# Mask products of the stick-breaking attention issued one step early, ahead of the scores they are added to

## The chip, the cores and the metric

The kernel runs on one core of one Trainium2 chip. The metric is the device time of one execution in microseconds (us), the median of several runs; lower is better.

## The reference

One residual block of a streaming encoder: 1024 tokens, width 1024, all in float32. A mixing sub-layer (retention and stick-breaking attention side by side, gated, projected and merged) is followed by a squared-ReLU MLP. Only the stick-breaking part matters here: 8 heads of 64, in blocks of 128 queries.

```python
z = jnp.einsum('bthd,bshd->bhts', q[:, t0:t1], k[:, :t1]) * scale
valid = s_idx[None, :] < t_idx[:, None]
log_1m = jnp.where(valid, -jax.nn.softplus(z), 0.0)
log_stick = lax.cumsum(log_1m, axis=3, reverse=True) - log_1m
a = jnp.where(valid, jnp.exp(jax.nn.log_sigmoid(z) + log_stick), 0.0)
outs.append(jnp.einsum('bhts,bshd->bthd', a, v[:, :t1]))
```

A query sees only earlier keys, so the 128x128 square on the diagonal needs a mask, and no other square does.

## The kernel before

The kernel is written engine by engine, each engine with its own program, and semaphores between them. The order in which TensorE works is written out by hand. In the stretch from about 59 to 313 us it works through the stick-breaking attention and, between its small products, through the dense projections that produce q, k, v and the gate (`stick_tile`, lines 610 to 612: three float32r products of 512 or 256 columns for each of 8 chunks).

**Units.** Two heads are taken together (a group G, 4 of them). For each group the 8 query blocks make 12 units: query blocks 0 to 3 are one unit each, and blocks 4 to 7 are two each, first the unit with the four newest key blocks (it holds the diagonal), then the rest. So 32 of the 48 units are diagonal (numbers 0, 1, 2, 3, 4, 6, 8, 10 of each group of 12) and 16 are not.

**Score banks.** The two heads of a unit U write PSUM banks (2U) mod 3 and (2U+1) mod 3. The second of these was last used by the first head of unit U-1. ScalarE reads a bank twice, L1051 (sigmoid of -z into `uu`) and L1052 (sigmoid of z into `sg`), and each read raises `sg_done` by one. `scores(U)` waits for `sg_done >= 4U-2`: both reads of the first head of the unit in front.

**One step U on TensorE:** transposes of the weights of unit U-2 (L645, waits for the product L1444 of VectorE, `a_done`), scores of unit U (L627, three passes of two row-tiled products, 64 rows each), for a diagonal unit the mask (L633: identity times a bfloat16 mask of 0 and -1e30, a full 128x128 product of 128 columns for each head, added onto the last 128 columns of the scores; it raises `z_done`), then the dense projection work that `STICK_BESIDE` lists for this step, then attention times v of unit U-2 (L663, 128x64 column tiles, waits for ScalarE's copy L1044, `at_ready`). `STICK_BESIDE` has no entry for steps 11, 23, 35 and 47: there times-v follows the scores at once. Steps 12, 24 and 36 open a new group.

**The other engines in a step.** ScalarE: copy of the finished output (L1039), copy `aT` (L1044), the four sigmoids of unit U, then evictions of dense tiles and the rounding of weight pieces (L973). VectorE: two scans (L1438, they wait for `sg_done`) and the product L1444. GpSimd computes the low parts of weight pieces (L449).

Of the kernel before, what the change touches and what calls it, by code (L numbers as in the profile page):

```python
# [8 lines left out]
P = 128  # L9
# [62 lines left out]
UNITS = tuple(u for i in range(T) for u in ([(i, 0, i + 1, True)] if i < 4 else [(i, i - 3, i + 1, True), (i, 0, i - 3, False)]))  # L72
N_UNITS = len(UNITS)
ALL_UNITS = 4 * N_UNITS
# [9 lines left out]
TILE_AT = {t: n for n, t in enumerate(STICK_TILE)}  # L84
# [3 lines left out]
LOW_AFTER = tuple(sum(t[0] in "qk" for t in STICK_TILE[:n]) for n in range(len(STICK_TILE) + 1))  # L88
# [63 lines left out]
def build_block(nc, x, wstream, ada, ada_rows, smalls, pos, ident, maskd, dprime, adab, postg, out, m1_dram, mods, x2_dram):  # L152
# [4 lines left out]
    with ctx:  # L157
        def sem(name):
            return ctx.enter_context(nc.semaphore(name))

        def sb(name, shape, dt, c=ctx):
            return c.enter_context(nc.sbuf_tensor(name, shape, dt))
# [47 lines left out]
        with ExitStack() as c:  # L210
# [9 lines left out]
            id_b = sb("id_b", [P, P], bf16, c)  # L220
            msk_b = sb("msk_b", [P, P], bf16, c)
# [51 lines left out]
        def chunk_bank(u):  # L273

            return ps[:, 2 + u % 6 if u < 8 else 4 + (u - 8) % 3, :]

        def x_slot(i):

            return xs[:, (i + 4) % T, :]
# [13 lines left out]
        def z_bank(x, w):  # L293

            return ps[:, x % 3, 0:w]
# [14 lines left out]
        qk_low, ada_half = sem("qk_low"), sem("ada_half")  # L310
        z_done, sg_done, scan_done, a_done = sem("z_done"), sem("sg_done"), sem("scan_done"), sem("a_done")
# [212 lines left out]
        def _(pe):  # L524
            def tile(outp, lhs, rhs, chunks, sem=gemm_done, ready=None):

                for k in range(chunks):
                    if ready:
                        pe.wait_ge(*ready(k))
                    (lh, ll), (rh, rl) = lhs(k), rhs(k)  # L530
                    nc.tensor.matmul(outp, lh, rh, start=(k == 0), stop=False)  # L531
                    nc.tensor.matmul(outp, lh, rl, start=False, stop=False)  # L532
                    last = nc.tensor.matmul(outp, ll, rh, start=False, stop=(k == chunks - 1))  # L533
                last.then_inc(sem, 1)
# [31 lines left out]
            def x_transposed(u):  # L566

                th, c = divmod(u, KC)
                if u in (0, 8):
                    pe.wait_ge(n1_x, 4 * (th + 1))  # L570
                if u in (6, 7):
                    pe.wait_ge(n1_split, 2 * (u - 5))
                if u >= 11:
                    pe.wait_ge(n1_split, 2 * (u - 2))
                for q in range(4):
                    last = nc.tensor.transpose(chunk_bank(u)[:, q * P:(q + 1) * P],
                                               x_slot(4 * th + q)[:, c * P:(c + 1) * P], id_f[:, :])
                last.then_inc(n1_tr, 1)
# [35 lines left out]
            def scores(U):  # L614

                G, k = divmod(U, N_UNITS)
                i, b0, b1, diagonal = UNITS[k]
                w = (b1 - b0) * P
                if k in (0, 4):
                    pe.wait_ge(qk_low, LOW_AFTER[TILE_AT["k", G, k // 4] + 1])  # L620
                if U:
                    pe.wait_ge(sg_done, 4 * U - 2)
                hi, lo = qk_hi[G % 2], qk_lo[G % 2]
                for n, (a, b) in enumerate(((hi, hi), (lo, hi), (hi, lo))):
                    for h in range(2):
                        rows_ = slice(64 * h, 64 * h + 64)
                        last = nc.tensor.matmul(z_bank(2 * U + h, w), a[rows_, 0, i * P:(i + 1) * P], b[rows_, 1, b0 * P:b1 * P],  # L627
                                                start=(n == 0), stop=(n == 2 and not diagonal))
                        if n == 2 and not diagonal:
                            last.then_inc(z_done, 1)  # L630
                if diagonal:
                    for h in range(2):
                        nc.tensor.matmul(z_bank(2 * U + h, w)[:, w - P:w], id_b[:, :], msk_b[:, :], start=False, stop=True).then_inc(z_done, 1)  # L633

            def weights_transposed(U):

                _, b0, b1, _ = UNITS[U % N_UNITS]
                pe.wait_ge(a_done, U + 1)
                if U:
                    pe.wait_ge(at_ready, U)  # L640
                for n in range(2 * (b1 - b0)):
                    h, b = divmod(n, b1 - b0)
                    for r in range(2):
                        part = slice(64 * r, 64 * r + 64)
                        last = nc.tensor.transpose(px[:, r, 64 * n:64 * n + 64], sg[part, U % 2, h, b * P:(b + 1) * P], id_f[part, part])  # L645
                        if n == 2 * (b1 - b0) - 1:
                            last.then_inc(at_tr, 1)
# [21 lines left out]
            def stick_tile(n, k0=0, k1=KC):  # L669

                kind, at, tok = STICK_TILE[n]
                piece = 3 * (at // 2) + 2 * (at % 2) if kind in "qk" else 3 * at + 1 if kind == "v" else PC_GATE
                slot = piece % 2
                if k0 == 0:
                    pe.wait_ge(w_split, 4 * piece + 4)
                    if n >= 4:
                        pe.wait_ge(*((ev_act, EA_STICK + n - 1) if STICK_TILE[n - 2][0] in "va" else (qk_low, LOW_AFTER[n - 1])))
                for k in range(k0, k1):
                    if kind == "v":
                        l, r_ = ((a[:, k, tok * P:(tok + 1) * P] for a in (a_hi, a_lo)), (w[:, slot, k * 256:(k + 1) * 256] for w in (w_hi, w_lo)))  # L680
                    else:
                        m, th = ("qk".index(kind), tok) if kind in "qk" else TT[tok]
                        l, r_ = ((w[:, slot, k * 256 + m * P:k * 256 + (m + 1) * P] for w in (w_hi, w_lo)),
                                 (a[:, k, th * HALF:(th + 1) * HALF] for a in (a_hi, a_lo)))
                    last = passes(tile_bank(n)[:, 0:256 if kind == "v" else HALF], *l, *r_, k == 0, k == KC - 1)
                if k1 == KC:
                    last.then_inc(gemm_done, 1)

            def gate_tile(j):

                m, th = TT[j]
                pe.wait_ge(w_split, 4 * (PC_GATE + 1) + 4)
                if j < 3:
                    pe.wait_ge(sg_done, 4 * ALL_UNITS - 4 + 2 * j)
                else:
                    pe.wait_ge(ev_act, EA_GATE + 3)
                tile(pg[:, j, :], lambda k: tuple(w[:, 1, k * 256 + m * P:k * 256 + (m + 1) * P] for w in (w_hi, w_lo)),
                     lambda k: tuple(a[:, k, th * HALF:(th + 1) * HALF] for a in (a_hi, a_lo)), KC)
# [6 lines left out]
                    x_transposed(6 + k)  # L705
            for u in CHUNKS_AFTER[1]:
                x_transposed(u)
            for U in range(ALL_UNITS + 2):
                if U == 2:
                    pe.wait_ge(n1_split, 32)  # L710
                if U >= 2:
                    weights_transposed(U - 2)
                if U < ALL_UNITS:
                    scores(U)
                for n, k0, k1 in STICK_BESIDE.get(U, ()):
                    stick_tile(n, k0, k1)
                    for u in CHUNKS_AFTER.get(n, ()):
                        x_transposed(u)
                if U >= ALL_UNITS:
                    gate_tile(U - ALL_UNITS)  # L720
                if U >= 2:
                    times_v(U - 2)

# [9 lines left out]
            for g in range(GATE_G):  # L733
                ea, ev = EA_GATE + 8 * g, EV_GATE + 8 * g
                n = PC_GATE + 3 * g
# [14 lines left out]
            def ret_group(g, sub, it):  # L750
# [41 lines left out]
                pe.wait_ge(ev_act, ea + 8)  # L792
                pe.wait_ge(w_split, 4 * (n + 2) + 4)
                scores(0)
                for i in range(T):
                    if i < T - 1:
# [1068 lines left out]
```

## Time and profile before

| | us |
|---|---|
| median of 3 runs (1763.54 to 1768.31) | 1764.07 |
| the profiled execution, its own time | 1766.35 |
| its span in the profile | 1764.5 |
| TensorE matmul busy (9968 products) | 1708.8 |
| VectorE busy | 906.4 |
| GpSimd busy | 602.3 |
| ScalarE busy | 560.7 |

The profile is one execution, taken by the hardware profiler. PE is TensorE's matmuls, PEld its weight loads, DVE VectorE, ACT ScalarE, POOL GpSimd. Lxxx is a line of the kernel. Matmuls overlap in the pipeline, so that the duration of one (start to modelled end) is longer than the distance from one start to the next, and it is mostly the distance that counts. The granted clock of TensorE is 0.99 of full speed over the span.

### The profile page before, as it was taken

The numbers are of one execution on the slowest core, as the hardware profiler recorded it, in microseconds if no ns is written. First come the engines' busy times: TensorE is split into PE (matmuls) and PEld (weight loads), VectorE is DVE, ScalarE is ACT, GpSimd is POOL, SyncE is SP. The second block draws the span as 40 slices with busy tenths as digits, with TensorE's granted clock in tenths as the row PEclk, the third lists the DMA queues.
The fourth block names the chain that finished last, engine by engine and source line by source line (L and its number), as shares of the span: only waits on it lengthen the run. The fifth ranks groups of instructions, "written<-read, shape, count | busy, mean of one in ns | idle before, by whom it ended". The sixth has DMA issues, their size and how long they took to land.

```text
span 1764.5 us, 25435 instructions
## 1 busy us (share of the span) xinstructions
PE 1708.8 (97%) x9968; PEld 1422.3 (81%) x9968; DVE 906.4 (51%) x1284; ACT 560.7 (32%) x949; POOL 602.3 (34%) x256
## 2 busy tenths in 40 slices
PE   4999999999999999999999999899999999999997
PEld 3877877777989898978888997788888888888876
DVE  6757666776456555542113277636261616253526
ACT  4556666110121212120002175333333333323232
POOL 2012111343332322323333742553535353444420
PEclk8999999999999999999999999999999999999999
DMA  9001001255401111113111545111111112020112
GB/s 362 1 25 49 18 32 61 96 203 168 147 28 49 37 40 45 39 42 124 45 46 48 187 160 179 48 48 49 48 59 36 61 35 71 24 85 16 66 77 114
DMA packets 38159, 135.16 MB, mean 77 GB/s; under 512 B 5940, under 2 KB 6836, under 8 KB 37560
## 3 DMA queue, kind: packets, MB, share of 16 engines
q1 hardware_dynamic: 30240, 109.66, 18.3%
q10 hardware_dynamic: 7832, 24.28, 3.7%
q8 instruction: 62, 1.02, 0.2%
q14 instruction: 25, 0.20, 0.0%
HBM read 121.33 MB, written 12.60 MB: 76 GB/s over the span
## 4 chain that ended last, share of the span: by engine, by line
PE 90%; DVE 5%; issue 1%; ACT 1%; DMA 1%; SPq 1%; POOL 0%; POOLq 0%; ACTq 0%; DVEq 0%
PE ps L533 17%; PE ps L531 17%; PE ps L532 16%; PE ps L906 5%; PE ps L908 5%; PE ps L907 5%; PE ps L610 3%; PE ps L611 3%; PE ps L612 3%; PE ps L786 2%; PE ps L663 2%; PE ps L788 2%; PE ps L787 2%; PE ps L627 1%; PE ps L645 1%
## 5 line engine op out<-in xcount | busy, mean ns | idle before, releaser
L438 POOL TENSOR_TENSOR w_hi<-raw,zero 128x1024 fp32r<-128x1024 f32 x58 | 114.3, 1970 | 468.1 <-PE ps L533 272.1
L533 PE MATMUL ps<-r_hi,w_lo 128*128 128x512 f32 x640 | 254.3, 397 | 0.0
L531 PE MATMUL ps<-r_hi,w_hi 128*128 128x512 f32 x640 | 252.2, 394 | 2.1 <-issue 2.1
L532 PE MATMUL ps<-r_lo,w_hi 128*128 128x512 f32 x640 | 252.0, 394 | 0.0
L531 PE MATMUL ps<-w_hi,a_hi 128*128 128x256 f32 x768 | 219.2, 285 | 1.3 <-POOL w_lo L467 0.7
L533 PE MATMUL ps<-w_hi,a_lo 128*128 128x256 f32 x768 | 215.7, 281 | 0.0
L532 PE MATMUL ps<-w_lo,a_hi 128*128 128x256 f32 x768 | 215.5, 281 | 0.0
L472 POOL TENSOR_TENSOR w_lo<-w,w_hi 128x1024 fp32r<-128x1024 f32 x39 | 100.0, 2564 | 221.3 <-ACT w_hi L1222 221.3
L1714 DVE TENSOR_TENSOR m<-m,ps 128x512 f32<-128x512 f32 x208 | 136.4, 683 | 71.2 <-PE ps L908 70.7
L906 PE MATMUL ps<-w_hi,f_hi 128*128 128x512 f32 x392 | 156.2, 398 | 4.8 <-issue 3.7
L907 PE MATMUL ps<-w_lo,f_hi 128*128 128x512 f32 x392 | 156.0, 398 | 0.0
L908 PE MATMUL ps<-w_hi,f_lo 128*128 128x512 f32 x392 | 155.9, 398 | 0.0
L531 PEld LDWEIGHTS ps<-w_hi,a_hi 128*128 128x128 f32 x768 | 144.9, 189 | 2.7 <-POOL w_lo L467 0.9
L440 POOL TENSOR_TENSOR w_lo<-raw,w_hi 128x1024 fp32r<-128x1024 f32 x58 | 144.8, 2497 | 4.5
L532 PEld LDWEIGHTS ps<-w_lo,a_hi 128*128 128x128 f32 x768 | 144.9, 189 | 0.2
L531 PEld LDWEIGHTS ps<-r_hi,w_hi 128*128 128x128 f32 x640 | 120.1, 188 | 30.7 <-issue 2.3
L533 PEld LDWEIGHTS ps<-w_hi,a_lo 128*128 128x128 f32 x768 | 144.7, 188 | 0.0
L532 PEld LDWEIGHTS ps<-r_lo,w_hi 128*128 128x128 f32 x640 | 120.1, 188 | 30.3
L533 PEld LDWEIGHTS ps<-r_hi,w_lo 128*128 128x128 f32 x640 | 120.1, 188 | 28.6
L1438 DVE TENSOR_TENSOR_SCAN uu<-uu 128x512 f32<-128x512 f32 (+7 forms) x96 | 96.1, 1042 | 77.1 <-ACT uu L1051 76.8
L1701 DVE TENSOR_TENSOR f_lo<-hid,f_hi 128x1024 fp32r<-128x1024 f32 x35 | 51.8, 1480 | 151.4 <-ACT f_hi L1249 151.4
L449 POOL TENSOR_TENSOR w_lo<-raw,w_hi 128x1024 fp32r<-128x1024 f32 x16 | 42.9, 2689 | 235.1 <-ACT w_hi L973 235.1
(232 smaller groups left out, 3427.8 us busy)
## 6 DMA issues: line engine op xcount, KB each, us to landing
raw<-wstream SPq DMA_DIRECT2D x112, 512.0 KB, 3.7
ada_r<-ada_rows SPq DMA_DIRECT2D x32, 512.0 KB, 4.9
w<-wstream SPq DMA_DIRECT2D x32, 512.0 KB, 3.7
ada_s<-ada SPq DMA_DIRECT2D x7, 1024.0 KB, 17.3
m_dram<-m1s ACTq DMA_DIRECT2D x1, 4096.0 KB, 15.6
m<-m_dram ACTq DMA_DIRECT2D x1, 4096.0 KB, 12.2
x_dram<-m ACTq DMA_DIRECT2D x8, 512.0 KB, 4.3
rl_f<-x_dram ACTq DMA_DIRECT2D x2, 2048.0 KB, 10.3
```

What stands on the lines that cost most here:

```text
L438: nc.gpsimd.tensor_tensor(w_hi[:, slot, part], raw[:, h, :], zero[:, 0:1].broadcast_to([P, RAW]), ALU.add).then_inc(w_split, 1)
L440: nc.gpsimd.tensor_tensor(w_lo[:, slot, part], raw[:, h, :], w_hi[:, slot, part].bitcast(f32), ALU.subtract).then_inc(w_split, 1)
L472: return nc.gpsimd.tensor_tensor(out_, in0, in1, op)
L531: nc.tensor.matmul(outp, lh, rh, start=(k == 0), stop=False)
L532: nc.tensor.matmul(outp, lh, rl, start=False, stop=False)
L533: last = nc.tensor.matmul(outp, ll, rh, start=False, stop=(k == chunks - 1))
L610: nc.tensor.matmul(outp, hi, r_hi_, start=start, stop=False)
L906: nc.tensor.matmul(banks[:, t, :], fh, wh, start=(start and c == 0), stop=False, skip_group_check=not start)
L907: nc.tensor.matmul(banks[:, t, :], fh, wl, start=False, stop=False, skip_group_check=not start)
L908: last = nc.tensor.matmul(banks[:, t, :], fl, wh, start=False, stop=(c == 1), skip_group_check=not start)
L1438: V.tensor_tensor_scan(run, run, run, 1.0, ALU.mult, ALU.bypass).then_inc(scan_done, 1)
L1714: V.tensor_tensor(dst, dst, bank, op).then_inc(ff_ev, 1)
```

## The change

Four things are edited. The mask products of a diagonal unit move out of `scores` into a function of their own, `mask_first`. They now open the accumulation in the bank (`start=True`, only in the last 128 columns), and the scores are added to them (`start=False` for a diagonal unit). `mask_first(U + 1)` is called in step U behind the dense work and in front of `times_v(U - 2)`; `mask_first(0)` stands ahead of the loop. The wait for `sg_done` goes with the mask: for a diagonal unit it now stands in `mask_first`, and the scores no longer have it. `z_done` of a diagonal unit is now raised by the last pass of the scores. Numbers of products, columns and operands are the same.

```diff
@@ scores(U)
-                if U:
+                if U and not diagonal:
                     pe.wait_ge(sg_done, 4 * U - 2)
...
                         last = nc.tensor.matmul(z_bank(2 * U + h, w), a[rows_, 0, i * P:(i + 1) * P], b[rows_, 1, b0 * P:b1 * P],
-                                                start=(n == 0), stop=(n == 2 and not diagonal))
-                        if n == 2 and not diagonal:
+                                                start=(n == 0 and not diagonal), stop=(n == 2), skip_group_check=diagonal)
+                        if n == 2:
                             last.then_inc(z_done, 1)
+
+            def mask_first(U):
+
+                _, b0, b1, diagonal = UNITS[U % N_UNITS]
+                w = (b1 - b0) * P
                 if diagonal:
+                    if U:
+                        pe.wait_ge(sg_done, 4 * U - 2)
+                    else:
+                        pe.wait_ge(qk_low, LOW_AFTER[TILE_AT["k", 0, 0] + 1])
                     for h in range(2):
-                        nc.tensor.matmul(z_bank(2 * U + h, w)[:, w - P:w], id_b[:, :], msk_b[:, :], start=False, stop=True).then_inc(z_done, 1)
+                        nc.tensor.matmul(z_bank(2 * U + h, w)[:, w - P:w], id_b[:, :], msk_b[:, :], start=True, stop=False, skip_group_check=True)
@@ the loop over steps
+            mask_first(0)
             for U in range(ALL_UNITS + 2):
...
                 if U >= ALL_UNITS:
                     gate_tile(U - ALL_UNITS)
+                if U + 1 < ALL_UNITS:
+                    mask_first(U + 1)
                 if U >= 2:
                     times_v(U - 2)
```

## Rows read from the trace of the kernel before

**Rows 1.** The page: the chain of work that ended last, by engine.
```profile
PE 90%; DVE 5%; issue 1%; ACT 1%; DMA 1%; SPq 1%; POOL 0%; POOLq 0%; ACTq 0%; DVEq 0%
```

**Rows 2.** Windows (one group's stretch): start:end, length, busy us by engine, PEclk, DMA share, GB/s.
```profile
133.00:193.00 60.00, 59.52 (x570) 47.25 (x568) 41.56 (x46) 36.92 (x80) 9.11 (x4) 1.00 0.12 36
```

**Rows 3.** Waits of PE, 55 to 340 us: waiting line, releaser, us in total, times, longest.
```profile
PE ps L645 <- DVE sg L1444: 2.3, 3, 1.7
PE ps L610 <- POOL w_lo L449: 1.9, 1, 1.9
PE ps L663 <- ACT aT L1044: 0.7, 4, 0.2
```

**Rows 4.** Line L633, the mask: durations in ns min/median/max, first and last start.
```profile
L633 PEld LDWEIGHTS ps<-msk_b,id_b x64: 95/97/99, 59.8 to 306.6; 128*128 128x128 bf16 x64
L633 PE MATMUL ps<-msk_b,id_b x64: 219/224/230, 59.8 to 306.7; 128*128 128x128 bf16 x64
```

**Rows 5.** Timeline of PE, step 8 (diagonal, 512 columns beside): start us, duration us, instruction.
```profile
116.20 0.40 PE L627 MATMUL ps<-qk_lo,qk_hi 64*128 64x512 f32 x2
116.53 0.29 PE L633 MATMUL ps<-msk_b,id_b 128*128 128x128 bf16 x2
...
119.29 0.39 PE L612 MATMUL ps<-a_hi,w_lo 128*128 128x512 f32 x1
119.61 0.66 PE L663 MATMUL ps<-aT,vs 128*64 128x128 f32 x8
```

**Rows 6.** Timeline of PE, step 9 (not diagonal, 512 columns beside).
```profile
121.34 0.34 PE L627 MATMUL ps<-qk_lo,qk_hi 64*128 64x384 f32 x2
...
124.28 0.40 PE L612 MATMUL ps<-a_hi,w_lo 128*128 128x512 f32 x1
```

**Rows 7.** Timeline of PE, steps 7 (not diagonal) and 22 (diagonal), 256 columns beside.
```profile
111.54 0.28 PE L627 MATMUL ps<-qk_lo,qk_hi 64*128 64x256 f32 x2
...
114.44 0.28 PE L611 MATMUL ps<-w_lo,a_hi 128*128 128x256 f32 x1
114.56 0.28 PE L612 MATMUL ps<-w_hi,a_lo 128*128 128x256 f32 x1
114.76 0.44 PE L663 MATMUL ps<-aT,vs 128*64 128x128 f32 x4
...
186.40 0.40 PE L627 MATMUL ps<-qk_lo,qk_hi 64*128 64x512 f32 x2
...
189.61 0.28 PE L612 MATMUL ps<-w_hi,a_lo 128*128 128x256 f32 x1
```

**Rows 8.** Timeline of all engines, step 11, which has no dense work beside.
```profile
131.36 0.81 ACT L1044 ACTIVATE aT<-ps 128x768 f32<-128x768 f32 x1 [0.24 <-PE ps L645]
131.65 0.40 PE L627 MATMUL ps<-qk_lo,qk_hi 64*128 64x512 f32 x2
132.22 0.88 PE L663 MATMUL ps<-aT,vs 128*64 128x128 f32 x12 [0.17 <-ACT aT L1044]
132.58 0.59 ACT L1052 ACTIVATE sg<-ps 128x512 f32<-128x512 f32 x1
133.03 0.71 PE L645 MATMUL ps<-id_f,sg 64*128 64x64 f32 x16
133.55 0.31 PE L627 MATMUL ps<-qk_hi 64*128 64x128 f32 x2
```

**Rows 9.** Timeline, step 12: ScalarE's second read, and the last dense product.
```profile
136.18 0.34 ACT L1052 ACTIVATE sg<-ps 128x128 f32<-128x128 f32 x1
...
137.46 0.40 PE L612 MATMUL ps<-a_hi,w_lo 128*128 128x512 f32 x1
```

**Rows 10.** Timeline of PE, step 13: the transposes of unit 11 wait for VectorE.
```profile
139.18 0.71 PE L645 MATMUL ps<-id_f,sg 64*128 64x64 f32 x16 [0.30 <-DVE sg L1444]
```

**Rows 11.** Windows behind the two longest idle times of PE in the stretch.
```profile
100.00:104.00 4.00, 3.91 (x11) 3.10 (x12) 1.06 (x3) 0.00 (x0) 0.04 (x1) 0.58 0.43 131
...
322.00:325.00 3.00, 2.71 (x25) 2.29 (x26) 0.23 (x1) 1.03 (x1) 0.00 (x0) 1.00 0.00 0
```

## The prediction

> **What bounds the kernel now.** I read the chain of waits first: 90% of the chain that ended last is TensorE's own work, so what counts is TensorE's issue time, and other engines only where TensorE waits for them [rows 1]. Next the windows over the attention stretch: in one group's 60 us TensorE has matmuls in flight for 59.52 us, VectorE is busy for 41.56 and ScalarE for 36.92 [rows 2]. Then TensorE's waits there: 4.9 us in all, of which the 1.9 us for a weight piece and 1.7 us of the 2.3 for VectorE are two single events [rows 3]. So there is almost no stall that an earlier mask could remove. What is left is the price of the mask on TensorE itself, at its old and at its new place, and the wait that moves with it. Nothing behind about 323 us is touched by the change; it only starts later or earlier.
>
> **The mask at its old place (removed).** The 64 products last 224 ns each [rows 4], but what they cost is the distance that they put between neighbours. In a diagonal step from the end of the scores (116.20 + 0.40 = 116.60) to the start of the last dense product (119.29) it is 2.69 us [rows 5]; in a step without mask and with the same 12 dense products it is 124.28 - (121.34 + 0.34) = 2.60 us [rows 6]. That is 0.09 us for both heads. With 24 dense products of 256 columns: 189.61 - 186.80 = 2.81 against 114.56 - 111.82 = 2.74, or 0.07 us [rows 7]. It is this cheap because the array is emptied between row-tiled scores and full-array work with or without the mask, and the mask goes in where that has already been paid. Taken: 32 units x 0.08 = **-2.6 us**.
>
> **The mask at its new place (added).** No trace has it there, so I build it from neighbours. Dense products of 256 columns start 0.12 us apart, and from the last of them to times-v, which uses the array in another shape, it takes 0.20 us: its duration less about 0.08 [rows 7]. With 512 columns it is 119.61 - 119.29 = 0.32 against a duration of 0.39, so 0.07 less [rows 5]. The exit costs the last product's duration less 0.07, whatever that product is. With the mask behind the dense work: one spacing to the first mask product (0.12), 0.07 to the second (a pair takes 0.29 for 0.22 each [rows 4, 5]), then the exit, 0.22 - 0.07 = 0.15. Sum 0.34 against 0.20, and without rounding 0.13 us more. With 512 columns the same 0.13, for spacing and exit grow alike. The first product of the kernel's mask, ahead of the loop, costs the pair and the exit, 0.07 + 0.15 = 0.22 us. There are 28 steps in which `mask_first(U + 1)` stands behind dense work: 28 x 0.13 + 0.22 = **+3.9 us**. Bounds: not under the 0.07 that the pair costs at its old place (28 x 0.07 = 2.0 us), and up to 0.22 us if the change from float32r to bfloat16 empties the array too (an exit of 0.32 in place of a spacing of 0.23, 0.09 more; 6.2 us). I take 0.13, since the way back, bfloat16 to float32r, shows no such gap: the whole mask costs 0.09 there [rows 5, 6].
>
> The Trainium skill (TensorEngine Tiling (Array Packing), Key Properties) says that a change of tiling mode drains TensorE. The trace agrees: each change of array shape takes the last duration less 0.07 us [rows 5, 7]. By that rule, too, the move saves nothing, since there are as many changes of mode after it as before; a reading in which the mask alone causes a drain would have promised 32 x 0.3 us, and the steps without mask refute it.
>
> **The wait that moves.** `mask_first(U + 1)` waits for both ScalarE reads of the first head of unit U. Queued behind it on TensorE are times-v of U-2, the transposes of U-1 and the scores of U+1, none of which need that bank before the scores; ScalarE waits for these for its output copy, `aT` and sigmoids. Behind dense work the wait is covered. The smallest cover is in step 12: the read ends at 136.52 and the last dense product starts at 137.46, 0.94 us later [rows 9], and the same in step 36; in the other 26 it is larger. In **steps 11, 23 and 35** there is no dense work, and the cover is gone. In step 11 the scores' last pass starts at 131.65, and the second read of the first head ends at 132.58 + 0.59 = 133.17 [rows 8]. The release takes about 0.05 us (`aT` ends at 132.17, times-v starts at 132.22). So the mask starts at 133.22, its second product at 133.29, and times-v at 133.44, against 132.22 now: 1.22 us later, the old 0.17 us wait for `aT` now hidden inside. The transposes and scores behind it were not waiting for anything (133.03 and 133.55 follow at once), so they move with it. Steps 23 and 35 repeat the pattern to 0.01 us. 3 x 1.22 = **+3.7 us**. The kernel before met this wait for free, because times-v and the transposes lay in between. Bounds 1.1 to 1.3 us each.
>
> **What is late next.** Part of it is given back. In step 13 the transposes of unit 11 sit idle for 0.30 us, 0.37 us beyond the usual gap, until VectorE has unit 11's weights [rows 10]; unit 11's scores are not late, so VectorE isn't either, and a later TensorE loses this wait. The same in step 37, nothing in step 25: **-0.7 us**. The wait of 1.7 us for unit 47 [rows 3] comes behind a chain that starts with its late scores and shifts as a whole, so I give nothing for it. The sooner `z_done` (the mask's 0.2 us no longer stand between scores and sigmoids) helps ScalarE, on which TensorE waits for 0.7 us in all, in steps with scores that have no mask [rows 3, 8]; nothing for it either. The 1.9 us wait for a weight piece hangs on ScalarE's work of its own step and shifts too. No DMA, and nothing on SP's or POOL's queue, is passed by the moved products.
>
> **Sum.** -2.6 + 3.9 + 3.7 - 0.7 = +4.3 us. Against the profiled execution's own 1766.35 that is 1770.6; the median of the runs is 2.3 us lower, so 1764.07 + 4.3 = **1768.4 us**, 0.24% slower. About 0.3%, or 5.3 us, is what a measurement of this kernel can tell from no change, so I call this within it.
>
> **Rivals.**
> (A) *The clock falls behind the new waits.* This is the one that ends clearly slower. After the idle 1.9 us in step 5, which small products precede, the granted clock over the next 4 us is 0.58, the lower of the two levels, 1.2 GHz, for most of it; 4.0 x 0.42 = 1.7 us are lost. After the 1.7 us wait at 320 us it stays at 1.00, 2.4 GHz [rows 3, 11]. The new waits leave TensorE idle for 133.22 - 132.05 = 1.2 us, shorter than either, but with small products on both sides and no dense ones. Once: 1764.07 + 4.3 + 1.7 = 1770.1; at all three: 1773.5. It decides the sign at the bound of 5.3 us: one fall is enough. For it: the small products around steps 11, 23 and 35. Against it: 1.7 us of idling was survived. Chance 0.22.
> (B) *The weight loads of the mask are not covered.* The Trainium skill (TensorE: Matmul & The Clock Gate, Part 3, The mechanism) says that a weight load overlaps running matmuls only where the row groups differ; the full-array mask load behind full-array products would then be exposed. In terms of rows: 2 loads of 97 ns at 28 places [rows 4] are 5.4 us more, 1773.8 us. Against it: dense products with the whole array for each start 0.12 us apart, and their loads can't stand between them at that distance [rows 7]. With the milder case, an emptied array between float32r and bfloat16 (28 x 0.09 = 2.5 us, 1770.9), chance 0.10.
> (C) *The waits don't cost what I say.* If something in front of the scores of units 12, 24 and 36 absorbs them, or the mask pair is as cheap at its new place as at its old one, the sum is between +0.6 and +2.6 us, 1764.7 to 1766.7. For it: ScalarE and VectorE have spare time after step 11 and TensorE waits for VectorE in step 13. Chance 0.15.
> (D) *A gain.* The sooner sigmoids take out the waits for ScalarE and VectorE and more (at most 3.0 us, [rows 3]) and the three waits stay small: 1762 to 1764. Chance 0.03; over 0.3% faster needs more than there is to take.
>
> **How the numbers follow.** The forecast has 0.50, (A) 0.22, (B) 0.10, (C) 0.15, (D) 0.03. Slower by over 0.3%: (A), most of (B), and a little of the forecast, whose bounds (+2 to +6) touch 5.3 us: 0.30. Faster by over 0.3%: 0.03. Within: 0.67. The range is from (C)'s middle, 1764.8, to (A) with three falls, 1773.5.
>
> **What would show each step.** In the trace after: L633's successor has no record of a wait except in steps 11, 23 and 35, where the mask waits for ACT L1052 by about 1.2 us each; times-v of step 11 starts 1.8 us behind the scores' last pass (now 0.57); in the other steps times-v starts 0.45 us behind the last dense product of 512 columns (now 0.32); from the scores' end to the last dense product of a diagonal step it is 2.60 us, not 2.69; the wait in step 13 is gone. The clock is 1.00 after steps 11, 23 and 35. The prediction is wrong if the mask pair behind dense work costs more than 0.2 us, if TensorE waits in steps other than these three, or if the clock falls there.

## The result and the profile after

The changed kernel takes 1769.99 us (median of 22 runs, 1766.23 to 1772.52), the kernel before 1764.31 us in the same comparison. The ratio is **1.0027, 95% interval 1.0021 to 1.0034**: 4.8 us slower, 3.7 to 6.0. A second comparison (10 runs of the changed kernel beside 23 of before) gave 1.0022, 1.0010 to 1.0034. The forecast was +4.3 us, within 0.3%; the range 1764.8 to 1773.5 holds the median.

The page of the profiled execution, its span 1769.7 us against 1764.5: first the span, then the share of the chain that ended last.
```profile
span 1769.7 us, 25428 instructions
...
PE 90%; DVE 5%; ACT 1%; issue 1%; DMA 1%; SPq 1%; POOL 0%; POOLq 0%; ACTq 0%; DVEq 0%
```
The bound is the same as in [rows 1]. The waits of TensorE between 55 and 345 us, the same view as [rows 3] (L654 is the old L645, L672 the old L663, L642 the mask):
```profile
PE ps L642 <- ACT sg L1064: 3.5, 3, 1.2
PE ps L610 <- POOL w_lo L449: 1.8, 1, 1.8
PE ps L654 <- DVE sg L1456: 1.7, 1, 1.7
PE ps L672 <- ACT aT L1056: 0.2, 1, 0.2
```
There is one new line, three waits of the mask for ScalarE's second read. Gone are two of the three waits for VectorE (0.6 us) and three of the four for `aT` (0.5 us). The wait for a weight piece in step 5 is 0.1 us shorter (1.89 before, 1.79 now). That is the sooner `z_done` at work: the mask of unit 4 no longer stands between its scores and its sigmoids, ScalarE's rounding behind them comes sooner, and GpSimd starts the low part of the piece 1.09 us ahead of the scores of unit 5 (97.65) instead of 0.98 (97.67). Before and after:
```profile
96.69 3.35 POOL L449 TENSOR_TENSOR w_lo<-raw,w_hi 128x1024 fp32r<-128x1024 f32 x1 [3.96 <-ACT w_hi L973]
96.56 3.36 POOL L449 TENSOR_TENSOR w_lo<-raw,w_hi 128x1024 fp32r<-128x1024 f32 x1 [3.93 <-ACT w_hi L985]
```
Step 11, as in [rows 8]:
```profile
130.25 0.40 PE L627 MATMUL ps<-qk_lo,qk_hi 64*128 64x512 f32 x2
...
131.18 0.59 ACT L1064 ACTIVATE sg<-ps 128x512 f32<-128x512 f32 x1
...
131.82 0.11 PEld L642 LDWEIGHTS ps<-msk_b,id_b 128*128 128x128 bf16 x2 [1.61 <-ACT sg L1064]
131.83 0.28 PE L642 MATMUL ps<-msk_b,id_b 128*128 128x128 bf16 x2 [1.18 <-ACT sg L1064]
132.04 0.88 PE L672 MATMUL ps<-aT,vs 128*64 128x128 f32 x12
...
132.85 0.71 PE L654 MATMUL ps<-id_f,sg 64*128 64x64 f32 x16
133.37 0.31 PE L627 MATMUL ps<-qk_hi 64*128 64x128 f32 x2
```
From the scores' last pass to times-v it is now 132.04 - 130.25 = 1.79 us, against 132.22 - 131.65 = 0.57 in [rows 8]; the scores of unit 12 follow 3.12 us behind that pass instead of 1.90. Steps 23 and 35 show the same 1.22 us.

Behind dense work the mask doesn't wait. Step 7 (256 columns, the place of [rows 7]) and step 12 (512 columns):
```profile
113.02 0.28 PE L612 MATMUL ps<-w_hi,a_lo 128*128 128x256 f32 x1
113.14 0.28 PE L642 MATMUL ps<-msk_b,id_b 128*128 128x128 bf16 x2
113.36 0.44 PE L672 MATMUL ps<-aT,vs 128*64 128x128 f32 x4
...
137.20 0.40 PE L612 MATMUL ps<-a_hi,w_lo 128*128 128x512 f32 x1
137.44 0.29 PE L642 MATMUL ps<-msk_b,id_b 128*128 128x128 bf16 x2
137.65 1.09 PE L672 MATMUL ps<-aT,vs 128*64 128x128 f32 x16
```
The first mask product starts 0.12 and 0.24 us behind the last dense one, the ordinary spacing of dense products, and times-v follows 0.22 and 0.21 us behind that. So 0.34 in place of 0.20, and 0.45 in place of 0.32: 0.13 us for the pair, as built from neighbours. At all 26 places where the mask stands right behind a dense product, times-v starts 0.45 or 0.34 us behind that product, to 0.01 us. At the old place there is now less, step 8 as in [rows 5]:
```profile
114.80 0.40 PE L627 MATMUL ps<-qk_lo,qk_hi 64*128 64x512 f32 x2
115.13 0.50 PE L610 MATMUL ps<-a_hi,w_hi 128*128 128x512 f32 x1
...
117.80 0.40 PE L612 MATMUL ps<-a_hi,w_lo 128*128 128x512 f32 x1
118.12 0.44 PE L672 MATMUL ps<-aT,vs 128*64 128x128 f32 x4
```
117.80 - 115.20 = 2.60 us, where it was 2.69. Why the pair is cheap at this place shows in the weight loads (PEld) of step 8, before and after:
```profile
116.53 0.11 PEld L633 LDWEIGHTS ps<-msk_b,id_b 128*128 128x128 bf16 x2 [0.37 <-issue]
116.60 0.19 PEld L610 LDWEIGHTS ps<-a_hi,w_hi 128*128 128x128 f32 x1
...
115.13 0.19 PEld L610 LDWEIGHTS ps<-a_hi,w_hi 128*128 128x128 f32 x1 [0.37 <-issue]
```
Behind the change of array shape the first load of 0.19 us has only the last 0.07 us of a running product (the scores) above it, and the second dense product follows the first by 0.34 us (115.47 - 115.13) instead of the usual 0.23. With the mask in front this load starts only 0.07 us later (0.40 in place of 0.33 us behind the scores' last pass), and the second mask product runs while it goes on. So the pair pushes the second dense product back by 0.08 us and not by the 0.13 that it costs behind dense work.

**Adding it up.** I measure the attention stretch from the first product of unit 0 (its mask in the changed kernel) to the first product of the gate tile behind the scores of unit 47. Before, and in the changed kernel:
```profile
59.34 0.33 PE L627 MATMUL ps<-qk_hi 64*128 64x128 f32 x2
...
313.69 0.50 PE L531 MATMUL ps<-a_hi,w_hi 128*128 128x512 f32 x1
...
58.97 0.29 PE L642 MATMUL ps<-msk_b,id_b 128*128 128x128 bf16 x2
...
316.25 0.49 PE L531 MATMUL ps<-a_hi,w_hi 128*128 128x512 f32 x1
```
That is 257.3 us; before it was 254.35, so 2.9 us more. But in before's trace the clock fell in step 5, the 0.58 of [rows 11], and here it did not, behind a wait of 1.79 us in place of 1.89 (windows 320 to 325 and 100 to 104 us, columns as in [rows 2]):
```profile
320.00:325.00 5.00, 3.29 (x30) 2.36 (x30) 4.76 (x2) 0.00 (x0) 3.63 (x2) 1.00 0.00 0
100.00:104.00 4.00, 4.00 (x30) 3.12 (x30) 0.94 (x3) 0.00 (x0) 0.00 (x0) 1.00 0.40 131
```
From the scores of unit 5 to those of unit 6 it takes 8.42 us before and 6.99 after. The kernels of e3, e7 and e9 below run the program of before up to this point, have no fall there and take 6.95 or 6.96 us: a fall costs about 1.5 us. (In the changed kernel the new mask pair and the shorter wait nearly cancel in this step.) Falls aside the stretch is **4.4 us longer**. Between the scores of unit 6 and those of unit 47, where neither trace has a fall, it is 209.04 against 205.02, 4.0 us more. The rest of the span's 5.2 us lies elsewhere: the stretch starts 0.4 us sooner after the start, and behind it the clock falls for longer in the changed kernel's trace (granted clock, the column behind POOL's, 0.91 and 1.00 before, 0.83 and 0.91 after):
```profile
780.00:800.00 20.00, 17.05 (x74) 13.77 (x74) 8.33 (x12) 3.08 (x5) 8.51 (x4) 0.91 0.17 53
1085.00:1105.00 20.00, 17.90 (x86) 14.54 (x85) 11.41 (x15) 11.73 (x18) 5.43 (x3) 1.00 0.26 79
...
780.00:800.00 20.00, 17.05 (x66) 13.49 (x65) 9.61 (x20) 3.01 (x6) 8.49 (x4) 0.83 0.16 54
1085.00:1105.00 20.00, 17.90 (x81) 14.45 (x80) 13.89 (x19) 12.28 (x19) 0.55 (x1) 0.91 0.23 79
```
From the end of the stretch on the changed kernel takes 2.6 us more, and the change has no work there.

### The profile page after: what moved, and what is told of

Same layout as the page of the kernel before. It is cut to its first block, busy times and chain, and to the rows that moved or that the text cites. A ratio compares the mean times of both kernels' runs of the same rounds, so it can differ in the third digit from the quotient of the medians.

```text
span 1769.7 us, 25428 instructions
## 1 busy us (share of the span) xinstructions
PE 1711.2 (97%) x9968; PEld 1424.1 (80%) x9968; DVE 905.8 (51%) x1284; ACT 560.8 (32%) x949; POOL 602.0 (34%) x256
## 4 chain that ended last, share of the span: by engine, by line
PE 90%; DVE 5%; ACT 1%; issue 1%; DMA 1%; SPq 1%; POOL 0%; POOLq 0%; ACTq 0%; DVEq 0%
PE ps L531 17%; PE ps L533 17%; PE ps L532 16%; PE ps L918 5%; PE ps L920 5%; PE ps L919 5%; PE ps L610 3%; PE ps L612 3%; PE ps L611 3%; PE ps L672 2%; PE ps L798 2%; PE ps L800 2%; PE ps L799 2%; PE ps L627 1%; PE ps L654 1%
```

## The experiments

The traces side by side. "Stretch" is as above. "6 to 47" is from the first product of unit 6's scores to the first of unit 47's. "Falls aside" takes 1.5 us for a clock fall that one of the two traces has in the stretch. What e9 gains at its last wait lies behind the stretch.

| kernel | stretch, us | fall in step 5 | 6 to 47, us | against before, falls aside | timed against before (95%) |
|---|---|---|---|---|---|
| before | 254.35 | yes | 205.02 | 0 | |
| changed | 257.29 | no | 209.04 | +4.4 | 1.0027 (1.0021 to 1.0034) |
| changed, again | 257.28 | no | 209.05 | +4.4 | 1.0022 (1.0010 to 1.0034) |
| e1 three masks left at their old place | 254.21 | no | 206.05 | +1.4 | 1.0006 (0.9997 to 1.0015) |
| e2 changed, dense work in steps 11, 23, 35 | 255.35 | yes | 205.65 | +1.0 | 0.9998 (0.9989 to 1.0007) |
| e3 before, the same dense work | 252.09 | no | 204.23 | -0.8 | 1.0003 (0.9994 to 1.0012) |
| e4 before without masks | 252.06 | yes | 203.20 | -2.3 | 0.9986 (0.9977 to 0.9995) |
| e5 changed, masks twice | 260.64 | no | 211.72 | +7.8 | one run |
| e6 before, masks twice | 257.64 | yes | 207.73 | +3.3 | one run |
| e7 before, the three waits alone | 255.13 | no | 207.31 | +2.3 | one run |
| e8 changed, wait for both heads | 263.06 | no, two later | 214.86 | +7.2 | one run |
| e9 e3, and half a gate tile in the last wait | 252.16 | no | 204.23 | -0.7 | 0.9981 (0.9971 to 0.9992) |

**e1: the wait undone, the move kept.**
```diff
+                late = diagonal and U in (12, 24, 36)
...
+                if late:
+                    for h in range(2):
+                        nc.tensor.matmul(z_bank(2 * U + h, w)[:, w - P:w], id_b[:, :], msk_b[:, :], start=False, stop=True, skip_group_check=True).then_inc(z_done, 1)
...
-                if U + 1 < ALL_UNITS:
+                if U + 1 < ALL_UNITS and U + 1 not in (12, 24, 36):
```


> The changed kernel, but units 12, 24 and 36 keep the mask behind their scores, so no mask stands where no dense work hides its wait. Theory (three exposed waits of 1.22 us, less 0.7 us given back, and 0.05 us a unit for the place of the pair): the waits for ScalarE's second read are gone from TensorE, the attention stretch (first scores of unit 0 to the first gate tile) is 1.5 us longer than before instead of 4.4, the 0.3 us wait for VectorE in steps 13 and 37 is back, and the kernel is 1.5 us slower than before. Rival (the pair is dear wherever it is moved, the waits are covered): still 3.5 to 5 us slower. Rival (clock falls behind the new waits cause it): 0 to 1.5 us slower, and the changed kernel's own trace would show falls there.

The stretch is 1.4 us longer than before (expected 1.5), with 29 of the 32 masks moved. TensorE's waits are before's again, those for VectorE 0.3 us shorter:
```profile
PE ps L659 <- DVE sg L1461: 2.0, 3, 1.7
PE ps L610 <- POOL w_lo L449: 1.8, 1, 1.8
PE ps L677 <- ACT aT L1061: 0.7, 4, 0.2
```
So three masks out of 32 carry 3.0 of the 4.4 us, and the other 29 carry 1.4, or 0.05 each, net of 0.3 us less waiting for VectorE and 0.1 less for the weight piece. "Dear wherever it is moved" is refuted; timed, the kernel can't be told from before (+1.1 us, -0.5 to +2.6).

**e7: the wait alone, nothing moved.**
```diff
+                if U in (11, 23, 35):
+                    pe.wait_ge(sg_done, 4 * U + 2)
                 if U >= 2:
                     times_v(U - 2)
```


> The kernel before, with nothing moved but the wait alone: in steps 11, 23 and 35 TensorE waits for both reads of the first head ahead of times-v. Theory: times-v starts 1.57 us behind the scores' last pass instead of 0.57, so 3 x 1.0 us more, and 0.7 us is given back in steps 13 and 37: +2.3 us in the stretch. Rival (the waits are absorbed further on): under 1 us.

+2.3 us, as expected. The wait in step 11, now in front of times-v:
```profile
130.50 0.88 PE L663 MATMUL ps<-aT,vs 128*64 128x128 f32 x12 [1.18 <-ACT sg L1054]
```
3 x 1.0 us come in and 0.7 go out: of the waits for VectorE only the 1.7 us one is left in this kernel too. e1 and e7 are the two parts of the change, and 1.4 + 2.3 = 3.7 of its 4.4 us. Of the missing 0.7 us, 3 x (0.22 - 0.07) = 0.45 are the three mask pairs that stand in the open behind the waits, and 0.3 us are what e1 has less of waiting for VectorE, which the whole change can't save a second time.

**e2 and e3: the cover restored by dense work.**
```diff
-    10: ((13, 0, 8),),
+    10: ((13, 0, 4),), 11: ((13, 4, 8),),
...
-    22: ((21, 0, 8),),
+    22: ((21, 0, 4),), 23: ((21, 4, 8),),
...
-    34: ((29, 0, 8),),
+    34: ((29, 0, 4),), 35: ((29, 4, 8),),
```


> The changed kernel, but half of the dense tile of steps 10, 22 and 34 (12 products of 256 columns, 1.4 us) is done in steps 11, 23 and 35, so that it stands between the scores and the next unit's mask. Theory: the cover of 1.4 us is about as long as the wait (mask ready 1.57 us behind the last pass), so the mask waits 0 to 0.1 us; the stretch is 1.5 us longer than before less up to 0.7 us, since the wait for the copy aT (0.25 us beyond the usual gap) is covered as well, but each step gets one more change of array shape (0.1 us); about +1.3 us. Rival (it is the place of the pair): no change against the changed kernel, +4 to +5 us.

> The kernel before, with the same redistribution of dense work as the run above and the masks at their old place. Theory: only the 0.25 us waits for the copy aT in steps 11, 23 and 35 can be gained, and 0.3 us in step 13 and 37, against a new way into and out of dense work of about 0.1 us each: between -1.5 and 0 us against before. If the redistribution alone gains 2 us or more, the run above tells nothing of the wait.

e2 is +1.0 us (expected +1.3), e3 is -0.8. In e2 the mask in step 11 follows its dense work without a wait:
```profile
132.38 0.28 PE L612 MATMUL ps<-w_hi,a_lo 128*128 128x256 f32 x1
132.51 0.29 PE L642 MATMUL ps<-msk_b,id_b 128*128 128x128 bf16 x2
132.72 0.55 PE L672 MATMUL ps<-aT,vs 128*64 128x128 f32 x6
```
1.4 us of dense work between two dependent steps take away a wait of 1.2 us and cost nothing in the trace, since they come from a neighbouring step. With that cover all 32 masks at their new place cost 1.8 us more than at the old one (e2 against e3, falls aside), with no wait in it. That is what the move costs by itself, read from one trace of each; the timed medians, 1765.13 us for e2 and 1765.50 for e3, are too coarse to show it.

**e4: no mask at all.**
```diff
-                if diagonal:
-                    for h in range(2):
-                        nc.tensor.matmul(z_bank(2 * U + h, w)[:, w - P:w], id_b[:, :], msk_b[:, :], start=False, stop=True).then_inc(z_done, 1)
```


> The kernel before with the 64 mask products left out (the upper triangles of the diagonal squares aren't masked; the last pass of the scores raises the semaphore). Theory: they cost 0.07 to 0.09 us a unit at their old place, 2.6 us in all; the stretch is 2.6 us shorter. Rival (they cost more, as the issue time of 64 separate products would have it, 64 x 0.07 = 4.3 us, or their 0.3 us a unit, 10 us): 4 to 10 us shorter.

-2.3 us, 0.07 for each pair; expected 2.6. The most that any placing of the mask could gain is 0.13% of the kernel.

**e5 and e6: each pair twice**, at the new and at the old place.
```diff
-                    for h in range(2):
-                        nc.tensor.matmul(z_bank(2 * U + h, w)[:, w - P:w], id_b[:, :], msk_b[:, :], start=True, stop=False, skip_group_check=True)
+                    for n in range(2):
+                        for h in range(2):
+                            nc.tensor.matmul(z_bank(2 * U + h, w)[:, w - P:w], id_b[:, :], msk_b[:, :], start=(n == 0), stop=False, skip_group_check=True)
```


> The changed kernel with each mask pair issued twice at its new place (the mask is added twice, -2e30 in place of -1e30, which the sigmoids can't tell). It measures the price of a pair by itself. Theory: a pair costs its own two spacings, 0.13 us, wherever nothing hides it: in steps with dense work times-v starts 0.58 us behind the last dense product of 512 columns instead of 0.45, and the stretch grows by 32 x 0.13 = 4.3 us against the changed kernel. Rival (the pair costs a drain of its own at float32r to bfloat16): the first pair is dear and the second is not, again 0.13 us; told apart by the first gap, which is 0.24 us if there is no drain and 0.33 if there is.

> The kernel before with each mask pair issued twice at its old place. Theory: the first pair is cheap there (0.07 to 0.09 us) because it stands in a gap that the dense work behind has anyway, where its first weight load isn't covered; the second pair has no such gap and costs the full 0.13 us, so the stretch grows by 32 x 0.13 = 4.3 us against before. Rival (a pair costs 0.08 us at this place whatever stands around it): 2.6 us.

The second pair costs 3.35 us in all at the new place and 3.3 at the old one, 0.10 to 0.11 us a unit at both. The size was expected at 0.13 (4.3 us) and missed: products that follow a pair are spaced at 0.055 us, the first two at 0.067. At the old place 3.3 us is even nearer to the rival's 2.6, so this total alone doesn't decide between the two. Step 8 of e6, as in [rows 5]:
```profile
115.43 0.40 PE L627 MATMUL ps<-qk_lo,qk_hi 64*128 64x512 f32 x2
115.76 0.40 PE L634 MATMUL ps<-msk_b,id_b 128*128 128x128 bf16 x4
115.97 0.48 PE L610 MATMUL ps<-a_hi,w_hi 128*128 128x512 f32 x1
```
Four products take 0.40 us where two took 0.29 [rows 5]. What decides is the comparison of the places: the first pair costs 0.07 us at the old one and 0.13 at the new one, the second pair the same at both. So only at the old place is part of a pair free, and the first pair uses it up.

**e8: a longer wait, to see the clock.**
```diff
-                        pe.wait_ge(sg_done, 4 * U - 2)
+                        pe.wait_ge(sg_done, 4 * U - (0 if U in (12, 24, 36) else 2))
```


> The changed kernel, with the masks of units 12, 24 and 36 waiting for both heads' reads of the unit in front, 0.97 us longer. Theory: 3 x 0.97 = 2.9 us more in the stretch, nothing given back (step 13's wait is already gone), and the idle time of 2.15 us in each of the three is longer than the 1.9 us of step 5. If the clock falls behind such waits as the rival has it, this run shows it in steps 11 to 13, 23 to 25 or 35 to 37, with 1.4 us for each fall; if it does not, the rival has little left.

5.8 us over the changed kernel: 3 x 0.97 = 2.9 from the wait, and 2.9 from two clock falls, in steps 11 and 23, none in step 35. The wait with the slow products behind it, and the windows around the three waits (granted clock is the column behind POOL's):
```profile
132.35 0.40 PE L642 MATMUL ps<-msk_b,id_b 128*128 128x128 bf16 x2 [2.16 <-ACT sg L1064]
132.68 1.55 PE L672 MATMUL ps<-aT,vs 128*64 128x128 f32 x12
134.16 1.12 PE L654 MATMUL ps<-id_f,sg 64*128 64x64 f32 x16
...
131.00:136.00 5.00, 3.65 (x37) 3.05 (x38) 4.97 (x3) 3.17 (x6) 3.39 (x2) 0.66 0.32 105
196.00:201.00 5.00, 4.91 (x42) 4.14 (x43) 3.42 (x6) 2.02 (x7) 0.00 (x0) 0.66 0.01 3
256.00:262.00 6.00, 3.84 (x65) 2.84 (x61) 4.49 (x4) 5.12 (x9) 3.36 (x2) 1.00 0.23 86
```
Twelve times-v products take 1.55 us at 1.2 GHz, 0.88 at 2.4 GHz. So the mechanism of rival (A) exists at these places, behind a wait of 2.16 us; behind the changed kernel's own 1.18 us it did not show.

**e10: the changed kernel again.**

> The changed kernel once more, beside the run above, for a second trace. Theory: the three waits of 1.22 us repeat to 0.02 us, the stretch is 2.94 us longer than before where neither execution has a clock fall in it that the other has not, plus 1.4 us for a fall in step 5 that only before's trace had; the clock doesn't fall in steps 11 to 13, 23 to 25 and 35 to 37. Rival (the clock falls behind the new waits in some executions): one of the three shows 1.4 us.

The stretch repeats to 0.01 us, the three waits too (3.5 us in all), and the clock stays up behind them.

**e9: a version that beats both.** The kernel of e3, masks at their old place, and half of the second gate tile in front of the transposes of unit 47, which wait 1.7 us for VectorE.
```diff
+                if U == ALL_UNITS + 1:
+                    gate_tile(1, 0, 4)
                 if U >= 2:
                     weights_transposed(U - 2)
...
                 if U >= ALL_UNITS:
-                    gate_tile(U - ALL_UNITS)
+                    gate_tile(U - ALL_UNITS, 0 if U == ALL_UNITS else 4)
```


> The kernel before (masks at their old place) with two waits of the attention stretch covered: the dense redistribution of steps 10/11, 22/23 and 34/35, and the first half of the second gate tile (12 products of 512 columns, 2.8 us) in front of the transposes of unit 47, which wait 1.7 us for VectorE. Theory (only waits that end last are worth a reordering): -0.9 us from the redistribution, as its trace showed, and -1.7 + 0.2 us (one more change of array shape) from the second, so that the third gate tile ends 2.4 us sooner than before, clock falls aside; 0.1 to 0.2% faster than before, about 0.35% faster than the changed kernel. Rival (what waits for the later transposes of unit 47 gives it back): no gain.

1762.50 us (median of 12 runs) against 1765.34: **ratio 0.9981, 0.9971 to 0.9992**, 3.4 us faster than before (1.4 to 5.1). Its only waits between 55 and 345 us:
```profile
PE ps L610 <- POOL w_lo L449: 1.9, 1, 1.9
PE ps L663 <- ACT aT L1053: 0.2, 1, 0.2
```
From the scores of unit 47 to the last times-v it is 16.04 us in place of 17.61, 1.6 us less, and with e3's 0.8 us the trace has 2.4 us less, clock falls aside, which the timed interval holds. That is as much as e4 gains by taking out every mask, from work that was already in the program, put where TensorE waited.

## Why the prediction was right

**The bound.** TensorE's own issue time: right. e4 shows what the whole mask is worth at its old place, 2.3 us.

**The old place, -2.6 us.** Slightly too much: e4 has 0.07 us a pair, 2.3 us. I took 0.08 from one reading each of 0.09 and 0.07; unit by unit, before against e4, a pair costs 0.04 to 0.09 us in nearly all, 0.07 in the mean.

**The new place, +3.9 us.** Right: 0.13 us in each kind of step, no gap at float32r to bfloat16, and no exposed weight load. Rival (B) is refuted: the first mask product comes at the spacing of dense products (0.24 and 0.12 us), so its load stands under the last of them, full array behind full array; the rule that the prediction names for this rival doesn't hold here. The exit behind the mask is 0.15 us, its duration less 0.07, and as many changes of array shape stand after the move as before it. The Trainium skill (TensorEngine Tiling (Array Packing), Key Properties) says that a change of tiling mode drains TensorE. The trace agrees: the last product's duration less 0.07 us passes at each change shown here, whatever stands in front of it.

**The wait that moves, +3.7 us.** Right in place, number and size: steps 11, 23 and 35, 1.22 us each, and no other. e7 made the wait without the move, e1 the move without the wait.

**What is late next, -0.7 us.** Right: the transposes of unit 11 and of unit 35 gave 0.37 and 0.36 us back, those of unit 23 nothing. That the wait for unit 47 moves along was right too (1.7 us still). The wait for `aT` in the three steps went inside the new wait, and is in the 1.22. Wrong was that the wait for a weight piece hangs on ScalarE's work of its own step: it hangs on the rounding in the step before, behind sigmoids that now come sooner, and gave 0.1 us back.

**The sum.** +4.3 forecast, +4.4 read from the trace with falls aside, +4.8 (3.7 to 6.0) timed. That the forecast is within 0.1 us is partly luck: the old place was taken 0.3 us too dear, and the 0.1 us at the weight piece was missing, with the opposite sign. Of the parts 3.0 us are the three exposed waits with their pairs, net of what was given back, and 1.4 us the place of the 29 others.

**Rival (A), the clock.** It did not happen, and its case was weighed with too little. I said that the 1.7 us wait at 320 us was survived; that was one trace. In the traces of this study that have that wait, the clock fell behind it in 4 of 11, and behind the wait in step 5 (1.7 to 1.9 us) in 4 of 12. Behind the new waits of 1.2 us it fell in none of 12 (four traces, three waits each), behind those of 2.2 us in e8 in 2 of 3. So one trace of before, with one wait survived, could not have shown that 1.7 us is sometimes too long. Where between 1.2 and 1.7 us it begins no run shows, and the waits differ in place as well as in length. A single fall cost about 1.5 us, not the 1.7 that was taken.

**Rival (C), absorbed.** Refuted by e7, where 0.7 of 3.0 us are absorbed and not more, and by the 0.13 us of the pair at its new place. **Rival (D), a gain.** `z_done` does come sooner, and all that TensorE gets from it is the 0.1 us at the weight piece in step 5.

**The absolute time.** The median came out 1.6 us above the forecast, and 5.7 above before's. The trace's stretch has 4.4. Both traces of the changed kernel have a lower granted clock around 785 and 1095 us than before's one trace. That isn't tied to the moved masks: the trace of e9, with the masks at their old place, has 0.83 and 0.91 there too (773 to 793 and 1078 to 1098 us), and e7's has 0.91 at the second place (1084 to 1104 us). Whether the change makes this more likely is not settled; the ratio's interval holds the 4.4 us without it.

**The range.** Its lower end, 1764.8 us, was called the middle of (C), but (C) runs from 1764.7 to 1766.7, so it is (C)'s lower end. The result doesn't hang on it.

## What to carry to other kernels

Before moving an instruction ahead of others on a saturated engine, list for each call what stands between the producer of its wait and the new place: 29 of the 32 waited for nothing and cost 1.4 us in all, three had no cover and cost 3.0. A small product can be cheapest where the array has just changed shape, because part of its time falls under the next product's weight load, which stands largely open there anyway: 0.07 us a pair here, against 0.13 behind dense work. And look first at what the saturated engine waits for: covering a few such waits was worth 2.4 us here, as much as all the work that was moved.

## What the runs showed of the hardware

- **Idle time and the clock.** The granted clock fell behind none of the 12 idle stretches of 1.2 us (steps 11, 23, 35), behind 4 of 11 of 1.7 us (unit 47), 4 of 12 of 1.7 to 1.9 us (step 5) and 2 of 3 of 2.2 us (e8). A fall costs about 1.5 us: 19.14 or 19.15 in place of 17.61 us from the scores of unit 47 to the last times-v in the four traces that have one there. The same program shows it in one execution and not in another: the trace of before has the fall in step 5, those of e3, e7 and e9, which are alike up to there, have not.
- **The run-to-run spread goes with the granted clock.** The 22 runs of the changed kernel lie at 1766.2 to 1766.5 us where its mean is 0.993 and at 1768.2 to 1772.5 where it is 0.990, all but one of these above 1770.7. A change of under 2 us is better read from the stretch in the trace, which repeated to 0.01 us, than from medians.
- **Exit from an array shape.** The next shape's first product starts the last product's duration less 0.07 us behind its start: 0.15 behind 128 bfloat16 columns, 0.20 behind 256, 0.32 behind 512.
